# The lower weight parts of a two-group encoder step on one core: GpSimd's subtraction cut into four column ranges

## The reference

```python
shift, scale, gate = jnp.split(jax.nn.silu(c) @ w_ada + b_ada, 3, axis=-1)
h = rmsnorm(x, g_norm) * (1 + scale[:, None]) + shift[:, None]
z = h @ w_in                        # 1024 -> 5096 columns, split among all heads
oa = mla_attend(...)                # low-rank q and kv, chunk-causal, 8 heads
ob = dsa_attend(...)                # top-k keys by an indexer, bias, 8 heads
ya = (oa * jax.nn.silu(ga)) @ w_oa
yb = (ob * jax.nn.silu(gb)) @ w_ob
m = jax.nn.sigmoid(ma) * ya + jax.nn.sigmoid(mb) * yb
x = x + gate[:, None] * (m @ w_out)
```

## Time and profile before

| | us |
|---|---|
| median of 3 runs | 1159.55 |
| lowest and highest | 1158.65, 1162.95 |
| the profiled execution, its own time | 1160.03 |
| its span in the trace | 1158.2 |
| PE busy | 1083.6 (94%) |
| DVE busy | 721.6 (62%) |
| ACT busy | 476.9 (41%) |
| POOL busy | 347.1 (30%) |
| of that, L1631, 112 instructions | 270.3, mean 2413 ns |

### The profile page before, as it was taken

How to read it: one execution, slowest core, us unless ns; L and a number is a source line. 1 busy time by engine, 2 the same in 40 slices (tenths; PEclk the granted TensorE clock), 3 DMA queues, 4 the chain that set the end, 5 groups by cost and what they waited for, 6 DMA issues and landing times.

```text
span 1158.2 us, 19942 instructions
## 1 busy us (share of the span) xinstructions
PE 1083.6 (94%) x7724; PEld 937.2 (81%) x7724; DVE 721.6 (62%) x1512; ACT 476.9 (41%) x1073; POOL 347.1 (30%) x208
## 2 busy tenths in 40 slices
PE   7699999999979999989999999999999999989995
PEld 4398896878858888879978979678777889879994
DVE  1535999554896556655666399975476324664656
ACT  4335545343434434523244453744244443451321
POOL 0235534031212222243334463503011231333340
PEclk9799999899979999989999999999999999998998
DMA  8344122211134434413533312221112122431332
GB/s 354 147 154 137 56 79 72 74 37 37 56 110 144 151 104 136 128 56 112 175 123 95 86 55 92 64 80 44 36 39 69 56 65 73 128 124 60 120 105 78
DMA packets 33490, 113.23 MB, mean 98 GB/s; under 512 B 4586, under 2 KB 5322, under 8 KB 31732
## 3 DMA queue, kind: packets, MB, share of 16 engines
q1 hardware_dynamic: 32068, 109.43, 29.1%
q10 hardware_dynamic: 1328, 2.53, 0.6%
HBM read 104.82 MB, written 7.12 MB: 97 GB/s over the span
## 4 chain that ended last, share of the span: by engine, by line
PE 84%; DVE 7%; ACT 4%; issue 2%; POOL 1%; POOLq 0%; DMA 0%; ACTq 0%; SPq 0%; DVEq 0%
PE pj L673 19%; PE pj L675 18%; PE pj L674 18%; PE po L959 4%; PE ps L885 3%; PE turned L928 3%; PE ps L898 2%; PE pj L833 2%; PE pj L807 1%; PE ps L902 1%; PE po L945 1%; PE pj L818 1%; PE ps L382 1%; PE ps L748 1%; DVE squares L1524 1%
## 5 line engine op out<-in xcount | busy, mean ns | idle before, releaser
L673 PE MATMUL pj<-h_hi,w_hi 128*128 128x272 f32 x1776 | 531.2, 299 | 27.2 <-DVE h_lo L1532 11.2
L675 PE MATMUL pj<-h_lo,w_hi 128*128 128x272 f32 x1776 | 518.9, 292 | 0.0
L674 PE MATMUL pj<-h_hi,w_lo 128*128 128x272 f32 x1776 | 516.4, 291 | 0.0
L1631 POOL TENSOR_TENSOR w_lo<-ring,w_hi 128x1024 fp32r<-128x1024 f32 x112 | 270.3, 2413 | 601.8 <-ACT w_hi L1046 601.5
L673 PEld LDWEIGHTS pj<-h_hi,w_hi 128*128 128x128 f32 x1776 | 340.6, 192 | 45.4 <-issue 27.2
L674 PEld LDWEIGHTS pj<-h_hi,w_lo 128*128 128x128 f32 x1776 | 341.0, 192 | 0.2
L675 PEld LDWEIGHTS pj<-h_lo,w_hi 128*128 128x128 f32 x1776 | 339.7, 191 | 0.0
L1046 ACT ACTIVATE w_hi<-ring 128x1024 fp32r<-128x1024 f32 x112 | 118.9, 1062 | 150.8 <-PE pj L675 136.5
L1481 DVE TENSOR_SCALAR probs<-probs,inv 128x128 f32<-128x128 f32 (+4 forms) x136 | 79.3, 583 | 4.8
L1468 DVE CUSTOM_DVE_ANT_0 logit<-ps,bias_p 128x128 f32<-128x128 f32 (+3 forms) x64 | 28.9, 488 | 84.2 <-PE ps L902 84.0
L1524 DVE CUSTOM_DVE_ANT_0 squares<-ring,silu_c 128x1024 f32<-128x1024 f32 x64 | 80.4, 1257 | 1.3
(11 more groups left out here) (254 smaller groups left out, 1355.8 us busy)
## 6 DMA issues: line engine op xcount, KB each, us to landing
ring<-in_wts SPq DMA_DIRECT2D x150, 512.0 KB, 3.5
wide<-in_ada SPq DMA_DIRECT2D x3, 1024.0 KB, 21.1
ring<-in_wts SPq DMA_DIRECT2D x6, 384.0 KB, 3.1
wide<-in_xT SPq DMA_DIRECT2D x1, 2176.0 KB, 7.8
wide<-in_xT SPq DMA_DIRECT2D x2, 1088.0 KB, 5.6
x_between<-wide ACTq DMA_DIRECT2D x8, 272.0 KB, 2.1
wide<-x_between SPq DMA_DIRECT2D x2, 1088.0 KB, 5.5
bias_p<-in_ada SPq DMA_DIRECT2D x2, 1024.0 KB, 9.9
```

The costliest lines, as they stand in the source:

```text
L673: pe.matmul(out, hi, h_hi[:, k, half(b)], start=(k == first), stop=False)
L674: pe.matmul(out, lo, h_hi[:, k, half(b)], start=False, stop=False)
L675: return pe.matmul(out, hi, h_lo[:, k, half(b)], start=False, stop=(k == stop))
L1631: pool.tensor_tensor(w_lo[:, slot, :], ring[:, ring_slot[splits[n]], :], w_hi[:, slot, :].bitcast(F32), ALU.subtract).then_inc(s_wlo, 1)
```

## The change

The subtraction of `rest` is made in four instructions of 256 columns, one behind the other, in place of one of 1024. Only the first has a wait ahead of it, and only the last raises `s_wlo`; so whoever waits on that semaphore waits for all four.

```diff
                         split[0] += 1
                         pool.wait_ge(s_whi, n + 1)
                         slot = n % 2
-                        pool.tensor_tensor(w_lo[:, slot, :], ring[:, ring_slot[splits[n]], :], w_hi[:, slot, :].bitcast(F32),
-                                           ALU.subtract).then_inc(s_wlo, 1)
+                        for part in range(4):
+                            cols = slice(part * SLOT // 4, (part + 1) * SLOT // 4)
+                            last = pool.tensor_tensor(w_lo[:, slot, cols], ring[:, ring_slot[splits[n]], cols],
+                                                      w_hi[:, slot, cols].bitcast(F32), ALU.subtract)
+                        last.then_inc(s_wlo, 1)
```

## The result

The changed kernel takes 1164.99 us, the median of 8 runs (1161.92 to 1166.03), beside 1159.44 (1158.54 to 1162.95, 8 runs) for the kernel before. The ratio is 1.0032, with a 95% interval of 1.0018 to 1.0046: a little slower, within what was called no change, and 6 us above the forecast. The profiled execution of after took 1164.28 us with a span of 1162.5 us, 4.3 us more than that of before.

A forecast was written before the change was run, and what follows sets the result against it. TensorE was taken as the bound, with 84% of the chain. Costs of 2.4 less gains of 3.0 made -0.6 us against 1160.03, so 1159.4, stated as 1159.0 for the median; range 1155.0 to 1163.8.

The forecast's parts named there:

- Costs of 2.4 us: Four exposed tiles 1.6 us, VectorE coming in between pieces 0.6, end of first layer 0.2; bounds 0.6 to 4.0.
- The four waits: TensorE's waits for the subtraction at qi 1 and wx 7, both layers: 0.4 us longer and 0.7 longer.
- Rival four: Pieces cost less, four take 2.4 us, gains as forecast: -2.4 us, 1157.2; chance 0.12.
- GpSimd's busy time: Sign of being right: GpSimd (POOL) busy some 390 us.
- the reserve: Tiles of wo and wx are subtracted 2.30 us before first use, which covers most of the longer subtraction.
- rival three: VectorE delays every piece, a tile takes 5.9 us, the cover of wo and wx is gone: +43 us, 1203; chance 0.04.
- Rival one: The port lock isn't let go between pieces, held-up operations wait 2.78 us: +3.9 us, 1163.5; chance 0.24.
- Gains of 3.0 us: Held-up VectorE operations on the chain wait for one piece only: 1.2 + 0.6 + 1.0 + 0.2 us.
- VectorE's operations near 304 and 316 us: L1481 and L1524, held up by subtractions in the first layer, end earlier: 0.6 and 1.2 us gained.
- The second layer's end of attention: TensorE's wait for the fourth L1532 gets shorter: 1.0 us gained.
- rival two: VectorE takes the port at each boundary for all it has ready: 8.8 us gained, -6.4 in sum, 1153; chance 0.10.
- a second stretch of half clock that appears or goes: Listed among signs of being wrong: would move the time by a microsecond or two without the other signs.

The follow-up runs named there:

- e17: The kernel before, whole subtractions, with idle matmuls in the 1.59 and 0.82 us waits: 1160.42 us, ratio 1.0006.
- e18: Four pieces on all but the four exposed tiles, idle matmuls in the 2.40 and 1.59 us waits, second comparison: 1154.82 us, 0.9951 of before.
- e1: The kernel before with four pieces only for the four tiles whose lower part TensorE waits for: 1165.02 us, ratio 1.0038.
- e9: The kernel before with 4 idle matmuls, 0.64 us, inside a first-layer product where nothing waits: 1165.56 us, ratio 1.0040.
- e4: The changed kernel with 14 idle matmuls in the 2.40 us wait ahead of the fourth key product: 1160.37 us, 0.9994 of before.
- e16: Four pieces on all but the four exposed tiles, idle matmuls in the 2.40 us wait only: 1157.85 us, 0.9977 of before.

## Why the prediction was wrong, point by point

- **Costs of 2.4 us: right.** A piece takes 0.69 to 0.70 us from start to start where nothing interferes (2.80 to 2.83 us for a tile), against 0.69. The four waits grew by 0.41, 0.61, 0.42 and 0.61, 2.05 in all, against 0.4 and 0.7. Rival four, cheaper pieces, is out.
- **GpSimd's busy time: too low.** 415.8 us against some 390. The tiles took 3.05 us in the mean (341.8 / 112) and not 2.78, since VectorE comes in between the pieces of most tiles. It lay in idle time: the reserve fell from 2.30 to 1.67 us and was never used up, so rival three is out.
- **Rival one, no release between pieces: out.** L1524 took 1.63 us and not 3.8. The Trainium skill, "GPSIMD Engine Reference", section "Instruction dispatch", says that consecutive instructions are no barrier between GpSimd's cores; the runs show that VectorE gets the port between two of them all the same. That agrees with what the Trainium skill, "SBUF — State Buffer", section "Who interferes with whom", says of the port, that it is held for a whole instruction.
- **Gains of 3.0 us: about right where I looked, and incomplete.** VectorE's operations near 304 and 316 us brought 2.5 (forecast 1.8), as much as the pair e17 and e18 shows with the clock alike; that the row from 300 to 352 ends at 2.1 is in part luck, since 1.2 more came by 336 us and half clock at 345 took 1.4. The second layer's end of attention brought 1.2 (1.0), and the first layer's wait went from 5.76 to 5.73 (nothing). The output stage's wait of 1.52 became 0.97 and 0.18 more behind it, 0.1 by the shift (0.1). But I followed only VectorE's operations ahead of waits that I had listed, and left out the index stages, 0.9 us each, where TensorE's list of waits has none, before or after. With the 2.05 of costs the waits' part of -3.4 means gains of some 5 us: more than forecast, and less than the 8.8 of rival two.
- **The step that failed: the sum has no term for TensorE's clock.** It took the clock as it was in before, and put "a second stretch of half clock that appears or goes" at a microsecond or two, outside the sum. One stretch behind the 1.59 us wait costs 3.1 us in e1 and e9 and 4.6 in after (3.1 with the one at 280 that went), one behind the 2.40 us wait 1.7, and there are four such places. The clock's rows of the ledger make +7.6 us together, more than all terms of the sum. Removing waits on VectorE merged two waits into one of 2.40 us, and half clock followed it in 7 of the 8 cases with an open 2.40 us wait, never behind the pair; that much belongs to the change (3.4 us by the traces; filling it gave back 4.6 in e4 and some 2.3 in e16). The rest, the stretches at 262, 280, 822 and 840 us, belongs to where TensorE's work lies, which any edit moves: a bare 0.64 us did the same.
- **Range and chances.** With the waits alone the time would be 3.4 us below before; with the clock it was 4.2 above in the profiled pair and 5.5 by the medians; plain delays gave +4.8, +5.2 and +13.7 us. A range of 8.8 us had no room for that. The ratio of 1.0032 still lies within 0.5%, where I had put 0.90.

The Trainium skill, "TensorE: Matmul & The Clock Gate", section "Why this matters for your kernels", warns of long idle gaps between bursts of matmuls. Here the clock fell behind waits of 1.59 and 2.40 us, and stayed up behind others of the same length, all shorter than the gaps that the page warns of; the measurement decides. The Trainium skill says on the same page, section "What's actually happening", that the activity monitor runs freely and doesn't start anew with the kernel, which fits two executions of the same program that differ by 2.1 us, and behind the start in the clock alone.

## What to carry to other kernels

Cut a GpSimd instruction that shares a port with VectorE into pieces only where the consumer of its result has a reserve, and leave it whole where TensorE waits for it. When an edit shortens or merges waits of a TensorE-bound kernel, read the granted clock behind every wait of over a microsecond, and try idle matmuls inside one that half clock follows: in the 2.40 us wait they gave time back, in the 1.59 us wait the old kernel gained nothing by them. Before you credit or blame an edit of a few microseconds, run the old kernel with a bare delay of a fraction of a microsecond: if that moves the time as much, the edit's own value must be read from the waits, or from a pair with even clocks.

## What was not expected of the hardware

- Half clock costs what the bound makes of it. From 321 to 335 us the first profile of before ran at 0.52 of the clock, the second at 0.76 (windows of both below), and the work behind it was shifted by nothing (0.01 us): TensorE waits for ScalarE there, 8.6 us in sum in the one and 10.9 in the other. At 262 us, where nothing waits, the same kind of stretch costs 3 us.

```profile
321.00:335.00 14.00, 10.69 (x45) 0.52 0.36 116
```
```profile
321.00:335.00 14.00, 9.25 (x51) 0.76 0.37 129
```

- The time doesn't follow the work: +0.64 us gave +4.8, +1.44 gave +5.2, +2.6 gave +13.7, and +1.95 on the changed kernel gave nothing or less.
- Cutting a GpSimd instruction costs little by itself: four pieces take 2.80 us from the first start to the next instruction's where one took 2.39, 0.14 for each further piece. VectorE coming in between costs more: it pushed a piece out to 1.72 us at most, as the view of the changed line in after says (ns min/median/max).

```profile
L1633 POOL TENSOR_TENSOR w_lo<-ring,w_hi x448: 718/738/1719, 27.2 to 1138.1; 128x256 fp32r<-128x256 f32 x150
```
